# Eight more tokens of an expert layer through gathered rows, with smaller gate chunks and one gate piece moved to ScalarE

## What is computed

```
def one_block(args):
    xb, eb, gb = args
    a = jnp.einsum("td,thkd->thk", xb, u[eb])
    act = gb * jax.nn.gelu(a)
    return jnp.einsum("thk,thkd->td", act, v[eb])
```

## Time and profile before

| | |
|---|---|
| median of 3 runs | 3095.04 us (3094.26 to 3099.95) |
| the profiled execution | 3093.42 us, its span 3091.6 us |
| mean granted clock of TensorE | 0.987 of full |
| busy: TensorE matmul, VectorE, ScalarE, GpSimd | 97%, 81%, 33%, 25% of the span |
| loop U, loop V | from 1040 to 2093 us, from 2093 us to the end |
| moved by DMA | 892.78 MB, 289 GB/s over the span |

### The profile page before, as it was taken

How to read it: one execution, slowest core, us unless ns; L and a number is a source line. 1 busy time by engine, 2 the same in 40 slices (tenths; PEclk the granted TensorE clock), 3 DMA queues, 4 the chain that set the end, 5 groups by cost and what they waited for, 6 DMA issues and landing times.

```text
span 3091.6 us, 42071 instructions
## 1 busy us (share of the span) xinstructions
PE 2983.9 (97%) x17413; PEld 2756.3 (89%) x17413; DVE 2519.2 (81%) x3122; ACT 1033.6 (33%) x1094; POOL 781.7 (25%) x348
## 2 busy tenths in 40 slices
PE   6899989889899999999999999999999999999999
PEld 5786765467778999999999999998999999999999
DVE  7996968666763589989989898774989898989895
ACT  5323234431222333333333333332333334333331
POOL 0000000000120013333123333331455454545440
PEclk9999989999999999999999999999999999999999
DMA  9621233267644468888678988997999999999994
GB/s 382 277 95 68 89 111 121 96 254 296 264 164 163 147 251 337 324 336 321 246 290 339 356 346 336 385 377 304 387 394 389 391 394 389 393 390 393 389 393 173
DMA packets 182547, 892.78 MB, mean 289 GB/s; under 512 B 15713, under 2 KB 77281, under 8 KB 85857
## 3 DMA queue, kind: packets, MB, share of 16 engines
q1 hardware_dynamic: 111666, 490.25, 42.6%
q0 software_dynamic: 46080, 335.56, 26.6%
q10 hardware_dynamic: 24624, 64.45, 5.3%
HBM read 835.67 MB, written 54.53 MB: 288 GB/s over the span
## 4 chain that ended last, share of the span: by engine, by line
PE 87%; DVE 8%; ACT 3%; DMA 1%; issue 1%; POOL 0%; SPq 0%; ACTq 0%; DVEq 0%; POOLq 0%; PEldq 0%
PE bank L1953 11%; PE bank L1954 11%; PE bank L1955 11%; PE bank L2012 10%; PE bank L2014 10%; PE bank L2013 10%; PE bank L1637 3%; PE bank L1639 3%; PE bank L1638 3%; PE bank L1988 2%; PE bank L1889 2%; PE bank L1888 2%; DVE ada_w L969 2%; PE bank L1887 2%; DVE w_lo L936 1%
## 5 line engine op out<-in xcount | busy, mean ns | idle before, releaser
L471 POOL DMA_INDIRECT u_row<-u_rows,urow_i x128 | 287.5, 2246 | 823.5 <-DVE u_row L1406 559.0
L2012 PE MATMUL bank<-wt_hi,w_hi 128*128 128x352 f32 x1360 | 439.6, 323 | 7.3 <-DVE w_lo L923 4.7
L1953 PE MATMUL bank<-act_hi,w_hi 128*128 128x352 f32 x1376 | 446.6, 325 | 0.0
L1954 PE MATMUL bank<-act_lo,w_hi 128*128 128x352 f32 x1376 | 445.2, 324 | 0.0
L2013 PE MATMUL bank<-wt_lo,w_hi 128*128 128x352 f32 x1360 | 438.6, 323 | 0.0
L2014 PE MATMUL bank<-wt_hi,w_lo 128*128 128x352 f32 x1024 | 330.5, 323 | 0.0
L1955 PE MATMUL bank<-act_hi,w_lo 128*128 128x352 f32 x1024 | 330.0, 322 | 0.0
L1955 PE MATMUL bank<-act_hi,low 128*128 128x352 f32 x1024 | 330.0, 322 | 0.0
L2014 PE MATMUL bank<-wt_hi,low 128*128 128x352 f32 x1024 | 329.3, 322 | 0.0
L482 POOL DMA_INDIRECT u_row<-v_rows,urow_i x96 | 250.5, 2609 | 238.8 <-DVE y_g L1552 228.8
L1406 DVE SCALAR_TENSOR_TENSOR u_row<-u_row,h2t 128x2048 f32<-128x2048 f32 x128 | 288.6, 2284 | 14.9 <-DMA u_row<-u_rows,urow_i 14.9
(11 more groups left out here) (348 smaller groups left out, 7200.2 us busy)
## 6 DMA issues: line engine op xcount, KB each, us to landing
ada_w<-wada SPq DMA_DIRECT2D x80, 1024.0 KB, 5.9
w_raw<-u SPq DMA_DIRECT2D x64, 1024.0 KB
raw<-u SPq DMA_DIRECT2D x64, 1024.0 KB
w_raw<-v SPq DMA_DIRECT2D x64, 1024.0 KB
raw<-v SPq DMA_DIRECT2D x64, 1024.0 KB
w_raw<-win SPq DMA_DIRECT2D x27, 1024.0 KB, 4.8
gelu_scratch<-gelu_s ACTq DMA_DIRECT2D x128, 176.0 KB
gate_scratch<-g_chunk ACTq DMA_DIRECT2D x11, 2048.0 KB, 12.1
```

What stands on the lines that cost most here:

```text
L471: pool.indirect_dma_start(u_row[n % 3][:], None, urow_d, bass.IndirectOffsetOnAxis(ap=col, axis=0)).then_inc(u_row_loaded[n % 3], 16)
L1953: pe.matmul(out, wh[:, k, :], HD(k), start=(k == 0), stop=False)
L1954: pe.matmul(out, wh[:, k, :], LD(k), start=False, stop=False)
L2012: pe.matmul(o, wh[:, 8 * e + d, :], th, start=begin is not None and e == 0, stop=False)
```

## The change

It makes the dense tokens 344 instead of 352 and the extra gathered tokens 40 instead of 32. The 40 are two groups: the last 32 as before (`XA`), and 8 (`XB`) laid out as 8 tokens x 16 experts, with their own copy of the activations (`h2x_b`, 16 more transposes in U), their own row sum (`y_b`) and their own spread of the tables over the partitions (three matmuls into bank 5 and four VectorE operations). There are 40 row steps of extra tokens in `u` and 40 in `v`; 32 of the `u` steps lie in U (`XU`), 8 in V, so V keeps 176. The gate chunk becomes 28 tokens, thirteen chunks in all, and `weigh` becomes two instructions. The product with the third gate piece moves from VectorE to ScalarE, as eight instructions (`gate_hots`). Cut to its core:

```diff
-TD = 352
+TD = 344
-GC = 32
-N_CH = TD // GC
+GC = 28
+XB = 8
+XA = XT - XB
+N_CH = -(-TD // GC)
-XU = 16
+XU = 32
...
             pool.wait_ge(rows_ready, 1)
-            pool.wait_ge(h2x_set, 4)
+            pool.wait_ge(h2x_set, 8)
...
+            act.activation(x_rep_b[:], x_keep[:, :, 0:XB].unsqueeze(2).broadcast_to([P, KD, P // XB, XB]), ACT.Copy).then_inc(x_rep_ready, 1)
...
+            def gate_hots(t):
+
+                u = t % 2
+                act.wait_ge(hot_eq_ready[u], t // 2 + 1)
+                for n in range(8):
+                    ins = act.activation(hot1[2][:, u, n // 2, :, n % 2], hot_eq[:, u, n // 2, :, n % 2], ACT.Copy,
+                                         scale=gate_r[:, 8 * t + n:8 * t + n + 1])
+                ins.then_inc(hot_gated[u], 1)
+
             def keep_hots(t):
-                chunk, at_, cb = t // 4, 8 * (t % 4), t // 4 % 2
...
+                    chunk, at_ = (2 * t + g) // 7, 4 * ((2 * t + g) % 7)
...
-                    for m in range(2 + (3 * h + b) % 2):
+                    for m in range(3 if b else 2):
                         dot(n_dot)
...
-            T_.step(dve.tensor_tensor(sel[:], ident[:, 0:XT], ident[:, XT:2 * XT], ALU.add))
-            T_.step(dve.tensor_tensor(sel[:], sel[:], ident[:, 2 * XT:3 * XT], ALU.add))
-            T_.step(dve.tensor_tensor(sel[:], sel[:], ident[:, 3 * XT:4 * XT], ALU.add))
+            T_.mark(dve.reduce_sum(sel_a[:], ident[:].rearrange("p (q t) -> p t q", t=XA), AX_X))
+            T_.mark(dve.reduce_sum(sel_b[:], ident[:].rearrange("p (q t) -> p t q", t=XB), AX_X))
+            T_.step(dve.reduce_sum(eighth[:], ident[:].rearrange("p (q t) -> p q t", t=XB), AX_X))
...
-            dve.wait_ge(tabt_ready, 3)
+            dve.wait_ge(tabt_ready, 4)
+            T_.step(dve.tensor_tensor(parts_b[:], bank[5][:, 0:3 * P].rearrange("p (c q n) -> p c q n", c=3, n=XB),
+                                      eighth[:].unsqueeze(1).unsqueeze(3).broadcast_to([P, 3, P // XB, XB]), ALU.mult))
+            T_.step(dve.reduce_sum(table_b[:], parts_b[:].rearrange("p c q n -> p c n q"), AX_X))
+            T_.mark(dve.scalar_tensor_tensor(out=urow_x[:, 0:XB], in0=table_b[:, 0, :], scalar=float(P), in1=table_b[:, 1, :], op0=ALU.mult, op1=ALU.add))
+            T_.step(dve.tensor_copy(gate_x[:, 0:XB], table_b[:, 2, :]))
...
-                for j in range(3):
-                    ins = dve.tensor_tensor(hot1[j][:, u], hot1[2][:, u], of_tokens(gate_c[j], tok), ALU.mult)
+                dve.wait_ge(hot_eq_ready[u], t // 2 + 1)
+                for j in range(2):
+                    ins = dve.tensor_tensor(hot1[j][:, u], hot_eq[:, u], of_tokens(gate_c[j], tok), ALU.mult)
...
-                for m in range(2 if t % 3 == 2 else 1):
-                    dot(n_dot)
+                for m in range(1 + t % 2):
...
-                w = wt[:].rearrange("p i (c t) -> p i c t", c=TD // GC)
-                dve.tensor_tensor(w, w, gate_l[:].rearrange("p c i t -> p i c t"), ALU.mult).then_inc(wt_ready, 1)
+                whole = GC * (N_CH - 1)
+                w = wt[:, :, 0:whole].rearrange("p i (c t) -> p i c t", t=GC)
+                dve.tensor_tensor(w, w, gate_l[:, 0:N_CH - 1].rearrange("p c i t -> p i c t"), ALU.mult).then_inc(wt_ready, 1)
+                dve.tensor_tensor(wt[:, :, whole:TD], wt[:, :, whole:TD], gate_l[:, N_CH - 1, :, 0:TD - whole], ALU.mult).then_inc(wt_ready, 1)
...
-                for m in range(2 if n % 2 else 1):
+                for m in range(2 if n % 4 else 1):
                     if n_dot < P:
                         dot(n_dot)
...
+            turn_x(x_rep)
+            for u in range(2, 4):
+                u_job(u)
+            pe.wait_ge(x_rep_ready, 2)
+            pe.wait_ge(h2x_set, 4)
+            turn_x(x_rep_b)
...
+            for t_i, tab in enumerate((e1_t, e2_t, gate_t)):
+                last = pe.matmul(bank[5][:, t_i * P:(t_i + 1) * P], spread_b[:], tab[:, GB - 1, :], start=True, stop=True)
...
-                            last = pe.matmul(bank[d][:, TD:T - P], y_x[:, cols], sel[:], start=True, stop=True)
+                            pe.matmul(bank[d][:, TD:TD + XB], y_b[:, cols], sel_b[:], start=True, stop=True)
+                            last = pe.matmul(bank[d][:, TD + XB:T - P], y_a[:, cols], sel_a[:], start=True, stop=True)
```

More of the change, by code:

```diff
@@ L220, in build @@
         keys = at("keys", 160, [P, PH_, 2, NKEY])
-        g_chunk = [at(f"g_chunk{s}", 112 + 16 * s, [P, NKEY, GC]) for s in range(2)]
+        g_chunk = [at(f"g_chunk{s}", 112 + 14 * s, [P, NKEY, GC]) for s in range(2)]
         u_row = [at(f"u_row{s}", 164 + 8 * s, [P, D]) for s in range(3)]
@@ L317, in build @@
         hot_ready = [sem(f"hot_ready{s}") for s in range(2)]
+        hot_eq_ready, hot_gated = ([sem(f"{n}{s}") for s in range(2)] for n in ("hot_eq_ready", "hot_gated"))
         hot_used = [sem(f"hot_used{s}") for s in range(4)]
@@ L840, in keep_hots @@
                                    ACT.Copy).then_inc(g_copied[g], 1)
-                if t % 4 == 3:
-                    for g in range(2):
-                        act.wait_ge(g_copied[g], LEAD + t + 1)
-                    act.dma_start(gate_d[chunk], g_chunk[cb][:]).then_inc(g_stored[cb], 16)
+                    if at_ == GC - 4 or 8 * t + 4 * g == TD - 4:
+                        act.wait_ge(g_copied[0], LEAD + t + 1)
+                        act.wait_ge(g_copied[1], LEAD + t + g)
+                        act.dma_start(gate_d[chunk], g_chunk[cb][:]).then_inc(g_stored[cb], 16)
@@ L846, in weigh_hi, with keep_x @@
             def weigh_hi(n):
-                act.wait_ge(wt_ready, n + 1)
+                act.wait_ge(wt_ready, 2 * n + 2)
                 act.activation(wt_hi[n % 4][:], wt[:], ACT.Copy).then_inc(wth_ready, 1)
-            gelu_job(0)
-            gelu_job(1)
-            act.wait_ge(h2x_ready, 4)
-            for j in range(4):
-                act.activation(h2x[:, 4 * j:4 * j + 4, :], bank[4 + j][:].rearrange("p (k t) -> p k t", t=P), ACT.Copy).then_inc(h2x_set, 1)
-            for u in range(2, NKEY):
+            def keep_x(part, to):
+                act.wait_ge(h2x_ready, 4 * part + 4)
+                for j in range(4):
+                    act.activation(to[:, 4 * j:4 * j + 4, :], bank[4 + j][:].rearrange("p (k t) -> p k t", t=P), ACT.Copy).then_inc(h2x_set, 1)
@@ L856, in _ @@
+            for u in range(NKEY):
                 gelu_job(u)
+                if u == 1:
+                    keep_x(0, h2x)
+                if u == 3:
+                    keep_x(1, h2x_b)
                 if u == TAB_G - 2:
@@ L1448, in _ @@
             T_.step(dve.tensor_copy(part[:], row_f[:]))
-            for q in range(P // XT):
-                rows, cols_ = slice(q * XT, (q + 1) * XT), slice(q * XT, (q + 1) * XT)
-                T_.mark(dve.tensor_copy(urow_x[rows, :], part[P - XT:P, cols_]))
-                T_.step(dve.tensor_copy(gate_x[rows, :], gate_t[P - XT:P, GB - 1, cols_]))
-            dve.sem_inc(rows_ready, 1)
-            T_.step(dve.tensor_tensor(sel[:], ident[:, 0:XT], ident[:, XT:2 * XT], ALU.add))
-            T_.step(dve.tensor_tensor(sel[:], sel[:], ident[:, 2 * XT:3 * XT], ALU.add))
-            T_.step(dve.tensor_tensor(sel[:], sel[:], ident[:, 3 * XT:4 * XT], ALU.add))
+            for q in range(P // XA):
+                rows, cols_ = slice(q * XA, (q + 1) * XA), slice(q * XA, (q + 1) * XA)
+                T_.mark(dve.tensor_copy(urow_x[rows, XB:XT], part[P - XA:P, cols_]))
+                T_.step(dve.tensor_copy(gate_x[rows, XB:XT], gate_t[P - XA:P, GB - 1, cols_]))
+            T_.mark(dve.reduce_sum(sel_a[:], ident[:].rearrange("p (q t) -> p t q", t=XA), AX_X))
+            T_.mark(dve.reduce_sum(sel_b[:], ident[:].rearrange("p (q t) -> p t q", t=XB), AX_X))
+            T_.step(dve.reduce_sum(eighth[:], ident[:].rearrange("p (q t) -> p q t", t=XB), AX_X))
             for m in range(2):
@@ L1608, in _ @@
                 if i == 0:
-                    dve.memset(y_x[:], 0.0).then_inc(y_x_set, 1)
+                    for y in (y_a, y_b):
+                        dve.memset(y[:], 0.0).then_inc(y_x_set, 1)
             for e in range(10):
@@ L1956, in u_job, with turn_x @@
                 last.then_inc(pe_jobs, 1)
+            def turn_x(rep):
+                for k in range(KD):
+                    last = pe.transpose(bank[4 + k // 4][:, (k % 4) * P:(k % 4 + 1) * P], rep[:, k, :, :].rearrange("p a t -> p (a t)"), ident[:])
+                    if k % 4 == 3:
+                        last.then_inc(h2x_ready, 1)
             for u in range(2):
@@ L1961, in _ @@
             pe.wait_ge(h2t_set, 4)
-            for k in range(KD):
-                last = pe.transpose(bank[4 + k // 4][:, (k % 4) * P:(k % 4 + 1) * P], x_rep[:, k, :, :].rearrange("p a t -> p (a t)"), ident[:])
-                if k % 4 == 3:
-                    last.then_inc(h2x_ready, 1)
-            for u in range(2, TAB + 7):
+            turn_x(x_rep)
```

(2 more changed lines are left out.)

81 lines of the change are left out of this document (52 added, 29 removed).

## The result

The changed kernel takes 3104.75 us (median of 10 runs, 3101.77 to 3108.69), the kernel before on the same chip 3094.82: ratio 1.0028, 95% interval 1.0019 to 1.0037. Measured again on another chip it was 1.0022 (1.0012 to 1.0033). It is slower by 7 to 10 us. The forecast was 3078, and the range ended at 3094: the prediction is wrong, in sign too. I compare stretches of the two traces, by the ends of jobs, which SyncE's queue shows (the load of a tile is issued at the end of the job four before it). "Forecast" is the prediction's own terms put in their stretch.

The account below looks back on a forecast made before the run. TensorE's columns were taken as the bound, VectorE becoming it in V with DMA as near. U 17.5 - 6 at its end + 4.4 in V = 15.9 us less than 3093.4: 3077.5, stated as 3078, range 3060 to 3094.

Parts of the forecast that it names:

- Columns in U: Loop U: eight columns less save 3.33 ns per matmul, 20.5 us in all; a job becomes 7.57 us.
- Selection: VectorE in U: groups of 2, 3, 3 dots average 14.6 us against two jobs of 15.14; no cost.
- Tables: U at tile 68: four operations on bank 5 take 1.5 us and stall TensorE once, 2.0 us (bounds 0 and 4).
- Gate steps on ScalarE: U's gate steps: eight small activations, 2 us together, in a step of about 6 of 8.96 us; hidden.
- The end of U: Last 16 jobs of U: 53.7 MB crowd DMA, 11.4 us too many; 6 us of new idle (bounds 0 and 12).
- V: Loop V: VectorE becomes the bound, DMA as near; 30.45 us per unit; 4.4 us gained after closing sums (19 gained to 8 lost).
- Rival A: TensorE stays the bound to the end: seam no worse, V at 29.92 us a unit, 3057 us; chance 0.18.
- Rival B: Gate packets of 448 bytes cost twice those of 512: V's unit 33.1 us, time 3155 us; chance 0.08.
- C: Rival: weight loading sets matmul spacing at 352, so columns give nothing and added work remains, 3100 us; chance 0.05.
- Closing: Closing jobs after V: 16 more small sum matmuls on the path, at 0.1 us each.

Follow-up runs that it names:

- the one with 24 rows: Changed kernel with the chunk, unit-load, tile 68, gate-step-order and row-spacing edits, 24 rows in U's last 16 jobs, 68 in gate steps: 3080.99 us, 0.9949 of before.
- the mended kernels with 28 and 21 rows at the end: Changed kernel with small last gate chunk, unit load, tile 68 low part and gate steps moved: 28 rows (weighted rows 352 apart) 3087.60 us; 21 rows 3089.57 us.

## Why the prediction was wrong

**Columns in U: right.** 0 to 64 to within 0.1 us, with the 16 transposes at their price.

**Selection: right.** No stall; the average over three groups held.

**Tables: right in place and cause, low in price.** The four operations on bank 5 took 1.94 us (I put 1.5), the stall 2.49 to 2.7 us (2.0). I did not count that TensorE can run at its half clock behind such a stall, which made it about 4.5 us in most traces.

**Gate steps on ScalarE: "hidden" failed.** Eight take 2.48 us (I took 2, bounds 0.8 to 4.7), and the step has room for that. But I costed them by their sum and not by their place in ScalarE's queue, behind the split of a tile that can be late. 2.7 us of the gate steps, shown by two runs. Another 2.3 us is that a set with its entry cost 1.45 us a step (9.02 less a job of 7.57) instead of 1.39; that was not tried further.

By the Trainium skill, "VectorE: DVE Perf Modes", in the section on the TRN2 errata, a ScalarE copy from SBUF costs 224 cycles plus its elements; for 128 elements at the page's 1.2 GHz that is an estimate of 293 ns. The trace agrees: the eight start 293 ns apart and take 2.48 us together, the last one's 0.43 us included.

**The end of U: the step that failed.** The bytes were right: 53.7 MB forecast for the 16 jobs, 54.4 moved (376 GB/s over the 144.7 us from the end of job 112 to that of job 128). They were put at 11.4 us too many at 405 GB/s. "Part of the 11.4 us is taken up by the three jobs that a tile is loaded ahead, and the queue drains at the seam. I take 6 us of new idle, bounds 0 and 12." Measured: 23.4 us over the stretch 112 to 136, twice the upper bound. Four things went wrong in it.

The rate was too high. 405 GB/s is what single full windows show, but the 16 jobs hold a part that isn't full (316 GB/s from 2078.2 us on), and the kernel before moved 379 over the same 16 jobs (125.5 us) with TensorE idle 0.6 us. At 379 the 54.4 MB are an estimate of 143.5 us, 22 too many and not 11.4, against 144.7 measured.

The queues had little room at its start. The gate steps moved 375 GB/s in their last four jobs (1936 to 1972.4 us; before 362) and up to 401 over 20 us. Two whole chunks were stored there 9 us apart, the second, at 1967.3 us, for 8 tokens; it took 21.7 us to land. A gather that began at 1964.84, 7.6 us ahead of the stretch, took 17.62 us. So the tiles loaded ahead took up none of it that I can find.

The lateness is passed on through an order: gather, dot, low part, and three buffers; in that order TensorE stood still 17.3 us more. An estimate from the dots: 28 rows at 5.0 us instead of 4.3 are 19 to 20 us late. In the run with seven rows less a row was wanted every 5.8 us, in the one with 24 rows every 5.0, and TensorE stood still 6.0 and 12.2 us in the stretch, against 24.9. No run had more than three buffers in U, so what is due to the bytes and what to the buffers stays open.

And in or behind the longer stalls TensorE ran at the half clock for a while, 6 us in all.

The price of a row is no constant: left out of the changed kernel a row gives 3.4 us, moved ahead 2.4 (16.6 / 7), and between the mended kernels with 28 and 21 rows at the end, measured on two chips, 1.7 ((207.9 - 196.1) / 7), where its bytes are 2.6.

**V: right that it would not get all its columns, wrong on who keeps them.** I had VectorE as the bound at 30.45 us a unit. It is 30.21, TensorE is busy in all of it, and VectorE 27.6: the cycle of 30.22 that I took for VectorE's own work held a wait for ScalarE of 2.38. What is missing to 29.92 is in the spacing of the matmuls themselves, 157.4 ns and not 155.8, a part of it in how far the rows lie apart; the rest was not found. VectorE is near all the same: at 30.04 us a unit a low part came 1.45 us late. Rival A named the right bound and too low a time. Rival B is dead: with packets of 448 bytes the unit moves 399 GB/s (before 393). So is C: two jobs of U fell from 15.47 to 15.15 us with the columns.

**Closing.** 2.6 us more instead of 0.3. TensorE from one transpose of the gathered sums to the next, the kernel before and the changed one:

```profile
3047.84 0.27 PE L2017 MATMUL bank<-ident,y_g 128*128 128x128 f32 x1
...
3048.66 0.27 PE L2017 MATMUL bank<-ident,y_g 128*128 128x128 f32 x1
```
```profile
3053.57 0.27 PE L2077 MATMUL bank<-ident,y_g 128*128 128x128 f32 x1
...
3054.60 0.27 PE L2077 MATMUL bank<-ident,y_g 128*128 128x128 f32 x1
```

One round went from 0.82 to 1.03 us: two small sums in place of one cost 0.21 more (the new one 0.14, and the old one behind it went from 0.14 to 0.22). I took 0.1. Sixteen rounds are 3.4 us, and two units of V at 0.35 less take 0.7 off: 2.7 us by this estimate, 2.6 measured.

In the sum of the first traces, 20.6 us were gained in U and at the seam and 8.5 in V, and 23.4 at the end of U, 5.0 in the gate steps, 2.8 at the tables and 2.6 at the closing went back: 4.7 slower. My range was too narrow above all because I bounded each loss by itself, while the largest ones drew on the same full DMA queues. That V's unit came out between the 30.2 and 30.6 us that I had named was luck, since VectorE did not hold it there.

## What to carry to other kernels

When rows or tiles are moved into a stretch, add up its bytes, and also those of the stretch ahead; if the first is over what the queues carry and the second near it, expect more than the excess, because each late transfer is passed on through an in-order engine and then through TensorE's clock. Balance such work over stretches before judging the change: the same work was 0.2 to 0.3% slower or 0.5% faster than before by where four rows, one load and two kinds of steps stood, how much one store wrote and how far rows lay apart. Take the rate for such a sum from a whole stretch like it, not from its fullest window. Ask of each small step what stands ahead of it in its queue, not only how long it takes.

## What the runs showed of the hardware that was not expected

TensorE behind the stall at job 68, second trace of the changed kernel:

```profile
1565.40 0.43 PE L2000 MATMUL bank<-act_hi,hi_side 128*128 128x344 f32 x1 [2.61 <-DVE low L956]
...
1566.93 0.48 PE L2000 MATMUL bank<-act_hi,hi_side 128*128 128x344 f32 x1
...
1570.35 0.32 PE L2000 MATMUL bank<-act_hi,hi_side 128*128 128x344 f32 x1
```

The same stretch in windows, from the end of the stall on, and the stall of 6.36 us in the first trace:

```profile
1565.40:1566.93 1.53, 1.53 (x10) 1.53 (x10) 1.53 (x3) 0.26 (x1) 0.00 (x0) 1.00 0.91 345
1566.93:1570.35 3.42, 3.42 (x14) 3.42 (x13) 3.42 (x4) 0.00 (x0) 0.00 (x0) 0.50 0.38 153
```
```profile
1988.58:1994.94 6.36, 0.00 (x1) 0.00 (x1) 4.56 (x4) 0.95 (x2) 1.99 (x1) 0.72 1.03 429
```

At job 68 the granted clock is full (2.4 GHz) for 1.5 us behind the end of the stall and only then half (1.2 GHz): 12 matmuls take 3.42 us, 285 ns each instead of 158. In the first trace, with 2.49 us of idle, it did not fall. So an idle of 2.6 us cost 4.1. In the longer stall it fell while TensorE still stood (0.72 on average).

The spacing of matmuls with 344 columns is 157.8 ns in U, 157.4 in V with rows 344 apart, and 156.4 with rows 352 apart. Why was not tried.

One core draws 381 to 422 GB/s in full stretches of 30 us here, and 429 over the 6.36 us above. By the Trainium skill, "Perfetto Trace Analysis", Roofline, a core that is active alone is bounded by its 16 DMA engines at about 435 GB/s and not by the share of 358; the trace agrees.
